# Three query rotations ahead of the context norm's root, a second buffer of output rows turned two units later, first chunks in two groups, and filler products on TensorE

## The reference

```
u = x * (1 + scale) + shift                      # scale, shift from c_act @ w_ada
proj = u @ w_in                                  # split into a, b, q_lat, kv_lat, k_rope, gates, merge
q  = rms_norm(q_lat) @ w_uq                      # 8 heads: 64 plain + 32 rotated elements
kv = rms_norm(kv_lat) @ w_ukv                    # 8 heads: 64 of k, 64 of v
q_pe, k_pe = apply_rope(...)                     # rotation by cos and sin of the position
o  = causal attention over blocks of 128 queries # 4 blocks x 8 heads
a: 31-tap causal convolution, norm, silu;  b: 3-tap convolution, gates
out = (g_a*y_a + g_b*y_b + g_c*y_c) @ w_o, then a layer norm
```

## Time and profile before

| | us |
|---|---|
| median of 3 runs | 2397.62 |
| runs | 2395.1, 2397.62, 2403.35 |
| the profiled execution, its own time | 2397.72 |
| its span | 2395.9 |
| PE busy in it | 2272.7 (95%) |
| DVE, ACT, POOL busy | 1471.2, 850.6, 1083.8 |

### The profile page before, as it was taken

The page is one execution under the profiler, slowest core; times in us unless marked ns, Lnnn a source line. Parts: engine busy times, 40 slices in busy tenths (PEclk is TensorE's granted clock), DMA queues, the critical chain, the costliest instruction groups (busy, mean ns, idle before and its releaser), DMA issues.

```text
span 2395.9 us, 29954 instructions
## 1 busy us (share of the span) xinstructions
PE 2272.7 (95%) x10774; PEld 1843.4 (77%) x10774; DVE 1471.2 (61%) x2340; ACT 850.6 (36%) x1383; POOL 1083.8 (45%) x1276
## 2 busy tenths in 40 slices
PE   6799999999989989999999999999999999999997
PEld 3588777888668877788868888877777877788885
DVE  5889956554578985755378756546765765433311
ACT  2343334222443333422254433334343343333322
POOL 1555436565346543656425444432344444233342
PEclk8999999999999999999999999999999999999999
DMA  8332224665143222354313223233334233122222
GB/s 302 119 119 80 71 68 145 213 199 163 48 163 93 76 66 75 132 176 146 106 52 105 79 95 108 76 114 106 99 95 141 88 118 98 44 72 73 75 71 70
DMA packets 93203, 259.80 MB, mean 108 GB/s; under 512 B 10128, under 2 KB 11536, under 8 KB 92944
## 3 DMA queue, kind: packets, MB, share of 16 engines
q1 hardware_dynamic: 71392, 210.23, 27.8%
q10 hardware_dynamic: 21680, 47.79, 5.6%
HBM read 237.01 MB, written 20.97 MB: 108 GB/s over the span
## 4 chain that ended last, share of the span: by engine, by line
PE 56%; issue 14%; POOL 12%; DVE 10%; ACT 2%; DMA 1%; ACTq 0%; POOLq 0%; DVEq 0%; SPq 0%
PE bank L2015 17%; PE bank L2016 17%; PE bank L2017 17%; POOL t L419 12%; DVE t L1717 2%; DVE t L1168 1%; PE bank L2104 1%; PE bank L2085 1%; PE bank L2386 1%; PE bank L2062 1%; DVE t L1172 1%; POOL t L429 1%; DVE t L1834 0%; DMA t<-blocks 0%; PE bank L2554 0%
## 5 line engine op out<-in xcount | busy, mean ns | idle before, releaser
L419 POOL TENSOR_TENSOR t<-t,t 128x256 fp32r<-128x256 f32 x1208 | 1027.5, 882 | 1195.2 <-ACT t L482 1194.9
L2015 PE MATMUL bank<-t,t 128*128 128x512 f32 (+1 forms) x3056 | 1176.5, 385 | 43.6 <-DVE t L1168 12.7
L2016 PE MATMUL bank<-t,t 128*128 128x512 f32 (+1 forms) x3056 | 1150.2, 376 | 0.0
L2017 PE MATMUL bank<-t,t 128*128 128x512 f32 (+1 forms) x3056 | 1147.5, 375 | 0.0
L2015 PEld LDWEIGHTS bank<-t,t 128*128 128x128 f32 x3056 | 581.5, 190 | 173.2 <-DVE t L1168 16.0
L2017 PEld LDWEIGHTS bank<-t,t 128*128 128x128 f32 x3056 | 580.4, 190 | 106.4
L2016 PEld LDWEIGHTS bank<-t,t 128*128 128x128 f32 x3056 | 581.5, 190 | 103.9 <-issue 4.2
L482 ACT ACTIVATE t<-t 128x1024 fp32r<-128x1024 f32 x302 | 317.1, 1054 | 307.3 <-PE bank L2017 255.6
L1232 DVE SCALAR_TENSOR_TENSOR t<-t,t,t 128x512 f32<-128x512 f32 x168 | 153.3, 931 | 108.1 <-DMA t<-w_ada 64.6
L1506 DVE SCALAR_TENSOR_TENSOR t<-t,t,t 128x512 f32<-128x512 f32 x240 | 210.3, 876 | 6.7
L1172 DVE SCALAR_TENSOR_TENSOR t<-t,bank 128x512 f32<-128x512 f32 x112 | 76.7, 685 | 159.4 <-ACT t L1125 60.4
(11 more groups left out here) (242 smaller groups left out, 1773.4 us busy)
## 6 DMA issues: line engine op xcount, KB each, us to landing
t<-blocks SPq DMA_DIRECT2D x306, 512.0 KB, 3.6
t<-w_ada SPq DMA_DIRECT2D x144, 256.0 KB, 2.8
t<-w_ada SPq DMA_DIRECT2D x20, 512.0 KB, 11.6
xm_park<-t ACTq DMA_DIRECT2D x16, 384.0 KB, 2.3
s_park<-t ACTq DMA_DIRECT2D x16, 384.0 KB, 2.3
t<-xm_park ACTq DMA_DIRECT2D x16, 384.0 KB, 4.4
t<-s_park ACTq DMA_DIRECT2D x16, 384.0 KB, 5.1
xc_park<-t ACTq DMA_DIRECT2D x16, 256.0 KB, 2.0
```

The source lines that it names most:

```text
L419: low = pool.tensor_tensor(w_lo[slot][:, part], w_raw[slot][:, part], w_hi[slot][:, part].bitcast(F32), ALU.subtract)
L2015: pe.matmul(out, wh, xh, start=start, stop=False)
L2016: pe.matmul(out, wh, xl, start=False, stop=False)
L2017: return pe.matmul(out, wl, xh, start=False, stop=stop)
```

## The change

Four edits, all in layers 0 and 1.

1. Rotations: DVE makes the root of the context norm after the third head's rotation instead of the second's. ACT no longer stops for `knH` after head 2: it splits the next weight block there and makes `knH` after head 5 and that head's split.
2. Output rows: `o_rows` becomes two buffers used in turn; blocks 0, 1 and 2 are turned at units 11, 19 and 27 (steps 12, 20 and 25) instead of 9, 17 and 25. DVE waits for the turn of block i-2 where it waited for that of i-1.
3. First chunks, where there are three (layer 0): in the second half of the tiles the first two chunks are finished for all four tiles, then the third.
4. Six products of a 128x128 tile of ones by itself, into bank 5, which nothing reads, behind each half of the scale in layer 0.

```diff
-        o_rows = at(R_L + 13 * T, [128, HEADS * VH])
+        o_rows = [at(R_L + (13 + i) * T, [128, HEADS * VH]) for i in range(2)]
...
 # ACT, query heads
                     evac(qf[0:NOPE, h, :], banks[Q_BANK[h % 4]][0:NOPE, :], (l, "q", h), None)
-                    if h == 2:
+                    if h in (2, 5, 7):
+                        split_to(B_UQ(l) + RING + (h + 1) * 3 // 8)
+                    if h == 5:
                         for j in range(2):
                             act.wait_ge(dve_done, Dn(l, "kn", j))
                             act.activation(knH[:, j, :], kv_lat[:, j, :], ACT.Copy).then_inc(act_done, a(l, "knH", j))
-                    if h in (2, 5, 7):
-                        split_to(B_UQ(l) + RING + (h + 1) * 3 // 8)
...
-                            if unit[0] > 1 and unit[0] % HEADS == 1:
+                            if unit[0] > HEADS and unit[0] % HEADS == 3:
                                 o_turn(unit[0] // HEADS - 1)
...
 # DVE
                     rotate(qf[64:96, h, :], banks[Q_BANK[h % 4]], l, "q_pe", h)
-                    if h == 1:
+                    if h == 2:
...
-                    if i and h == 0:
-                        wp(l, "o_t", i - 1)
-                    dve.tensor_scalar(o_rows[:, h * VH:(h + 1) * VH],
+                    if i >= 2 and h == 0:
+                        wp(l, "o_t", i - 2)
+                    dve.tensor_scalar(o_rows[i % 2][:, h * VH:(h + 1) * VH],
...
 # PE
-                for k in range(KT):
-                    if k == KT // 2 and middle:
+                order = [(k, range(len(out))) for k in range(KT)]
+                if len(out) == 3:
+                    order[KT // 2:] = [(k, range(2)) for k in range(KT // 2, KT)] + [(k, (2,)) for k in range(KT // 2, KT)]
+                for i, (k, chunks) in enumerate(order):
+                    if i == KT // 2 and middle:
...
+            def ones_products(bank, n):
+
+                for _ in range(n):
+                    pe.matmul(banks[bank][:, 0:128], ones[:], ones[:], start=True, stop=True)
+
             pe.wait_ge(dve_done, Dn("c_act"))
             first_scale(0)
+            ones_products(5, 6)
...
+                first_scale(1)
+                ones_products(5, 6)
...
-                    pe.wait_ge(act_done, A(l, "probs_t", min(8 * i + 8, 31)))
+                    pe.wait_ge(act_done, A(l, "probs_t", min(8 * i + 10, 31)))
...
-                            tile_done = u > 1 and u % HEADS == 1
+                            tile_done = u > HEADS and u % HEADS == 3
                             if tile_done:
                                 turn_outputs(u // HEADS - 1)
```

More of the change, by code:

```diff
@@ L2042, in first_chunks @@
             def first_chunks(out, b, labels, ready, xh=uH, xl=uL, middle=None):
-                for k in range(KT):
-                    if k == KT // 2 and middle:
+                order = [(k, range(len(out))) for k in range(KT)]
[3 more added lines that the diff above has]
+                    if i == KT // 2 and middle:
                         middle()
                     pe.wait_ge(dve_done, ready(k))
-                    for n, bank in enumerate(out):
+                    for n in chunks:
+                        bank = out[n]
                         if k == 0:
@@ L2132, in first_scale, with second_scale @@
                 mm.then_inc(pe_done, p("ada_columns", half))
+            def ones_products(bank, n):
+                for _ in range(n):
+                    pe.matmul(banks[bank][:, 0:128], ones[:], ones[:], start=True, stop=True)
             pe.wait_ge(dve_done, Dn("c_act"))
             first_scale(0)
+            ones_products(5, 6)
+            def second_scale():
+                first_scale(1)
+                ones_products(5, 6)
             for l in range(L1):
@@ L2140, in _ @@
                 first_chunks(first, B_QL(l), [(l, "q_lat", j) for j in range(3)],
-                             lambda k: Dn(l, "uL", k), middle=(lambda: first_scale(1)) if l == 0 else None)
+                             lambda k: Dn(l, "uL", k), middle=second_scale if l == 0 else None)
                 if l:
@@ L2230, in turn_outputs @@
                     pe.wait_ge(dve_done, Dn(l, "o", 8 * i + 7))
-                    pe.wait_ge(act_done, A(l, "probs_t", min(8 * i + 8, 31)))
+                    pe.wait_ge(act_done, A(l, "probs_t", min(8 * i + 10, 31)))
                     for c in range(NA):
-                        mm = pe.transpose(banks[5][:, c * 128:(c + 1) * 128], o_rows[:, c * 128:(c + 1) * 128], ident[:])
+                        mm = pe.transpose(banks[5][:, c * 128:(c + 1) * 128], o_rows[i % 2][:, c * 128:(c + 1) * 128], ident[:])
                     mm.then_inc(pe_done, p(l, "o_t", i))
```

## The result

| | kernel before | changed kernel |
|---|---|---|
| median of the runs | 2398.51 us (2395.1 to 2403.35, 6 runs) | 2407.43 us (2403.86 to 2409.75, 6 runs) |
| profiled execution, its span | 2397.72, 2395.9 us | 2409.75, 2408.0 us |

The ratio is 1.0028, with the interval [1.0018, 1.0039]; a repeat gave 1.0029 [1.002, 1.0038]. The forecast was 2397.5 us and no change: it was wrong. The range ended at 2402.0. By the ratio the change costs some 7 us; the two profiled executions happen to lie 12 us apart, and where the other 5 come from is taken up under "The sum".

The account below looks back on a forecast made before the run. PE, busy 95% of the span, was taken as the bound, so only its idle and low-clock time could be won. Terms: -1.8 - 2 x 0.2 + 2 x 1.0 = -0.2 against 2397.72, so 2397.5 us; range 2391.0 to 2402.0.

Parts of the forecast that it names:

- Filler, -1.8 us: Layer 0's first chunks: filler products keep the clock full, first half at full clock; -1.8 us (bounds 0 and -2.2).
- starts it 1.8 us earlier: Layer 0's chain from the first chunks to the query heads: DVE paces it and starts it 1.8 us earlier.
- Rotations, -0.2 a layer: Query heads 6 and 7: the stall moves from head 6 to head 7; -0.2 us a layer (bounds +0.3, -1.0).
- Turns, +1.0 a layer: Turns at steps 12 and 20: PE waits for o_turn, clock falls; +1.0 us a layer (bounds -1.2, +1.7).
- by pace 1.0 earlier: Step 20: DVE's 1.12 us pause in step 19 goes, so PE gets bank 5 1.0 us earlier.
- a delay of 0 to 0.4. DVE hides this turn: Step 12: despite PE's wait and clock fall, its next chunk reaches DVE only 0 to 0.4 us late.
- Rival D: Step 12: PE's stop exceeds DVE's slack, delaying DVE and step 20; some +4.7 us a layer, 2405 us; chance 0.05.
- Rival C: All waits at the turns go, 7 us a layer, and heads give 1 each; 2380 us, 2389 if half; chance 0.09.

Follow-up runs that it names:

- e18: Changed kernel with its third turn (block 2's rows) back at the second unit of the next block; ratio to the kernel before 1.002.
- e14: Changed kernel with ACT's copy of turned rows ahead of the exponent, plus six products of ones at step 12 and twelve at step 20; ratio 1.0006.
- e2: Kernel before with only the rotations of three heads ahead of the root; ratio 0.9994.
- e10: Changed kernel with products of ones ahead of PE's wait for the turned rows: twelve at step 12, twenty at step 20, none at step 28; ratio 0.9997.
- e1: Kernel before with only the second output-row buffer and the later turns (steps 12, 20, 25); ratio 1.0021.
- e4: Changed kernel with ACT's copy of the turned outputs ahead of the exponent of its step; ratio to the kernel before 0.9983.
- e16: The same kernel as e4 (changed kernel, copy ahead of the exponent), run again; ratio to the kernel before 0.9983.
- e5: Changed kernel with twelve products of ones ahead of PE's wait at each of the three turns; ratio to the kernel before 1.0028.
- e6: e4 without the rotations, so kernel before with the start edit and later turns, copy ahead of the exponent; ratio 0.9993.

## Why the prediction was wrong

**Filler, -1.8 us: the mechanism is there, the gain is not reliable.** The clock from 32 to 36 us was full, against 0.55; it was 0.99 or 1.00 in ten of the twelve profiled executions with the filler (0.54 in e18, 0.50 in e14) and 0.50 to 0.78 in the seven without. Counted from the first product of the chunks, the changed kernel's trace even has the forecast gain: the second half comes after 18.05 us (20.16 before), the query heads after 60.92 (63.02) and the first score addition after 104.47 (106.24). But this execution began the chunks 1.6 us late (32.64 against 31.04), so little of it is seen in its times. And the gain doesn't come each time: from the first chunk to the first score addition the repeat took 105.96 us and the start-only run 107.89, since DVE there waited 2.96 us, in place of 1.33, for a load of `w_ada` in `products` (line 1232, at 101 us). The mean is 105.9 us over the twelve executions with the filler and 106.6 over the seven without, 0.7 us apart where single ones differ by 4. The step that failed is "starts it 1.8 us earlier", taken as certain; what it is worth in the median stays open (+0.2, +1.2, -2.2 and -3.6 us by the four comparisons, each with an interval of some 3 us). That the load's pace takes up the gain in the start-only run is what its trace suggests; no run moved that load.

**Rotations, -0.2 a layer: right mechanism, too good a size.** Head 6 waits 0.98 us and head 7 4.77 (forecast 4.8), and the edit alone is 0.9994 [0.9984, 1.0004], which covers -0.4 us and +1.0 alike. The traces speak against a gain: from the first rotation to the first score addition e2 takes 41.99 us in layer 0 and 40.44 in layer 1, against 41.73 and 39.68 before. Head 7 went on 0.8 us later than forecast (20.31 us behind the first rotation, against 19.5), and 0.7 of that are two of DVE's instructions ahead of it, which took 0.99 and 1.11 us with POOL now at work beside them, where the same ones took 0.68 and 0.75. The two `knL` tiles took 1.29 us together with POOL idle, 0.64 each; this agrees in kind with the port pair that DVE and GpSimd share in the Trainium skill (SBUF — State Buffer, "Who interferes with whom").

**Turns, +1.0 a layer: right mechanism, wrong size.** The waits came as foretold, 3.51 us (3.3) and 4.46 (3 to 4.4), four times, with the clock down behind each; a fall cost PE 1.4 to 2.8 us, 2.1 in the mean (2.0). Two steps failed. The first is "by pace 1.0 earlier", the credit for PE's better pace: with the clock held (e10) the landmarks are -0.1 and +0.1, so it is nothing. DVE's pause of 1.12 us in step 19 did go, but POOL's work came to stand beside DVE's there. DVE's timelines of step 19, changed kernel and before:

```profile
265.32 4.72 DVE L1506 SCALAR_TENSOR_TENSOR t<-t,t,t 128x512 f32<-128x512 f32 x5
...
270.68 1.22 DVE L1573 TENSOR_TENSOR t<-t,t 128x512 f32<-128x512 f32 x1
```

```profile
264.40 3.89 DVE L1506 SCALAR_TENSOR_TENSOR t<-t,t,t 128x512 f32<-128x512 f32 x5
...
270.13 0.69 DVE L1573 TENSOR_TENSOR t<-t,t 128x512 f32<-128x512 f32 x1
```

These take 1.36 us more, while POOL's four pieces of line 419 run from 267.63 on (before, from 270.39); line 1168 behind them takes 0.46 less, and step 20 comes 0.3 us earlier and not 1.1. That POOL slows them is read from the traces; no run moved its work. The second is "a delay of 0 to 0.4. DVE hides this turn", by which only the fall at step 20 was priced, 2.0 for each layer. Against e10 the changed kernel has lost 0.4 us by step 20 in layer 0 and 1.8 in layer 1, and 2.0 and 4.3 by the end of the layer. So in layer 0 that price held; in layer 1, where the clock stayed low longer, both falls were paid. In e1, with the same waits, the split is 3.0 and 2.9: what a fall costs in one layer differs from kernel to kernel. The term was +2.0 for both layers; the landmarks show +6.3 (+6.0 in the repeat), e1 alone measured +5.0.

**The sum.** The ratio of 1.0028 is 6.8 us, and the landmarks of the turns make up 6.3. The profiled executions lie 12.0 us apart, which falls into -0.2 up to the first score addition, +0.9 and +0.2 from there to step 12 in the two layers, +6.3 between the landmarks, +4.9 between the end of layer 0's attention and the start of layer 1's, and -0.1 behind. Of the 4.9 (5.6 in the repeat), 0.8 lies in layer 1 behind the first rotation, as above. The rest is no mark of the change: the whole stretch is 0.9 to 6.1 us longer in all others except e1 and e2 (2.6 and 1.1 less), also in those that are not slower. There PE waits for a weight block or the squares, and behind the longer waits the clock falls. What sets these waits in a given kernel stays open. Rival D named this very mechanism, PE's stop at step 12 longer than DVE's slack, with 2405 us and a chance of 0.05: it was the nearest case, and far too cheap a chance for a margin of some tenths of a microsecond. Rival C's gain was reached in part: with the copy first 2.4 us a layer (in three of the four layers of e4 and e16), not 7.

## What to carry to other kernels

A wait on TensorE has two prices, its length and the low clock behind it, and the second is paid only where TensorE is the late engine; so ask where the idle time will stand, not only how much there is. When a step is moved, look at what stands ahead of it in each engine's queue: one copy behind an exponent that waits for another engine made TensorE's waits at the turns 18.1 us, where they had been 13.6 (7.7 for the output rows and 5.9 for the copy), and the change was to shorten them. A forecast slack of 0.4 us held in one layer and not in the other, so it is a risk and not a cover. A gain that passes three engines and a load stream is to be counted over several executions, from the same first instruction to its last reader; and work moved away from one place stands beside other work at the next.

## What the runs showed that I had not expected

- Twelve and twenty small products of ones, which compute nothing, in front of four waits made the kernel 7.8 us faster with the waits' ends unmoved.
- The same stop and the same queue gave different lengths at the low clock: 1.42 us lost at step 12 in layer 0, 2.79 at step 12 in layer 1.
- The same start code met a granted clock of 1.00 from 28 to 30 us in the changed kernel's execution and of 0.50 in its repeat.
- In the changed kernel's trace the clock fell while TensorE worked on the second filler itself (its products go from 0.28 to 0.42 us at 48.7), and in the repeat it was 0.50 from 47.0 to 49.6 us, with PE busy 2.60 of 2.60 us. Only three of the twelve executions with the filler kept it at 1.00 from 48 to 52 us (e5, e6, e10).
- The same pause of 1.38 us at step 19 was followed by a fall in one execution of the copy-first kernel (e4) and by none in another (e16).
